# Recurrence heads of a group collected and turned by VectorE one block later, in a fused attention and recurrence block

## The reference

```python
h = rmsnorm(x, norm_gain[l])
proj = jnp.einsum('bsd,dn->bsn', h, w_in[l])
qa, ka, va, za, qb, fb, ib, zb, ga, gb = jnp.split(proj, SPLIT_POINTS, axis=-1)
a = window_sink_attention(qa, ka, va, attn_sinks[l]) * jax.nn.silu(za)
ob = hgrn2_chunkwise(qb, fb, ib, lower_bounds[l])
ob = ob * lax.rsqrt(jnp.mean(ob * ob, axis=-1, keepdims=True) + EPS)
ob = ob.reshape(B, S, HGRN_V_WIDTH) * hgrn_norm_gain[l].astype(jnp.float32)
b = ob.astype(x.dtype) * jax.nn.silu(zb)
y = (jax.nn.sigmoid(ga) * jnp.einsum('bsc,cd->bsd', a, w_up_attn[l])
     + jax.nn.sigmoid(gb) * jnp.einsum('bsc,cd->bsd', b, w_up_hgrn[l]))
x = x + jnp.einsum('bsd,de->bse', y, w_out[l])
```

## Time and profile before

| | |
|---|---|
| Median of 3 runs | 2672.86 us (2672.34 to 2673.23) |
| The profiled execution | 2672.82 us, of which its span of instructions is 2671.0 us |
| TensorE busy | 2642.4 us, 99% |
| VectorE busy | 1740.4 us, 65% |
| ScalarE busy | 1448.0 us, 54% |
| Granted clock of TensorE | 0.998 over the span |

### The profile page before, as it was taken

The page is one execution under the profiler, slowest core; times in us unless marked ns, Lnnn a source line. Parts: engine busy times, 40 slices in busy tenths (PEclk is TensorE's granted clock), DMA queues, the critical chain, the costliest instruction groups (busy, mean ns, idle before and its releaser), DMA issues.

```text
span 2671.0 us, 39981 instructions
## 1 busy us (share of the span) xinstructions
PE 2642.4 (99%) x12049; PEld 2195.7 (82%) x12049; DVE 1740.4 (65%) x3341; ACT 1448.0 (54%) x2420; POOL 0.2 (0%) x4
## 2 busy tenths in 40 slices
PE   8999999999999999999999999999999999999997
PEld 7788888888888888888888888888888888888886
DVE  6566887877877866666555656565656565755554
ACT  5555665656656555555544444444454544554544
POOL 0000000000000000000000000000000000000000
PEclk9999999999999999999999999999999999999999
DMA  7666565665656656666666666666666666676665
GB/s 235 183 194 177 169 183 172 174 182 168 179 173 174 182 173 174 180 177 178 175 189 199 190 195 191 195 190 195 190 195 190 195 191 193 196 221 211 213 214 179
DMA packets 258936, 503.39 MB, mean 188 GB/s; under 512 B 15552, under 2 KB 15760, under 8 KB 258832
## 3 DMA queue, kind: packets, MB, share of 16 engines
q1 hardware_dynamic: 258608, 502.02, 63.0%
q10 hardware_dynamic: 224, 0.03, 0.0%
HBM read 497.80 MB, written 4.19 MB: 188 GB/s over the span
## 4 chain that ended last, share of the span: by engine, by line
PE 97%; DVE 2%; ACT 0%; DMA 0%; issue 0%; SPq 0%; ACTq 0%; DVEq 0%
PE acc L398 31%; PE acc L402 31%; PE acc L399 31%; PE lev L411 1%; DVE w_lo L847 1%; PE lev L413 0%; DVE land_h L855 0%; DMA x_in<-in_x_dram 0%; DVE h_lo L1192 0%; PE mis L424 0%; DVE proj L855 0%; PE mis L458 0%; PE lev L450 0%; ACT w_hi L584 0%; PE outp L435 0%
## 5 line engine op out<-in xcount | busy, mean ns | idle before, releaser
L847 DVE TENSOR_TENSOR w_lo<-raw,w_hi 128x512 fp32r<-128x512 f32 x1856 | 1274.0, 690 | 886.1 <-ACT w_hi L584 880.5
L584 ACT ACTIVATE w_hi<-raw 128x512 fp32r<-128x512 f32 x1856 | 1164.1, 631 | 1166.6 <-PE acc L402 1153.6
L398 PE MATMUL acc<-w_hi,h_hi 128*128 128x512 f32 x3200 | 1263.0, 395 | 2.5 <-ACT w_hi L584 2.5
L399 PE MATMUL acc<-w_hi,h_lo 128*128 128x512 f32 x3200 | 1247.3, 390 | 0.0
L402 PE MATMUL acc<-w_lo,h_hi 128*128 128x512 f32 x3200 | 987.4, 390 | 0.2
L402 PEld LDWEIGHTS acc<-w_lo,h_hi 128*128 128x128 f32 x3200 | 600.4, 188 | 129.1 <-DVE w_lo L847 2.4
L398 PEld LDWEIGHTS acc<-w_hi,h_hi 128*128 128x128 f32 x3200 | 601.5, 188 | 124.0 <-ACT w_hi L584 3.3
L399 PEld LDWEIGHTS acc<-w_hi,h_lo 128*128 128x128 f32 x3200 | 601.7, 188 | 120.9
L398 PE MATMUL acc<-w_hi,a_hi 128*128 128x512 f32 x256 | 99.6, 389 | 0.0
L399 PE MATMUL acc<-w_hi,a_lo 128*128 128x512 f32 x256 | 99.6, 389 | 0.0
L398 PE MATMUL acc<-w_hi,b_hi 128*128 128x512 f32 x256 | 99.6, 389 | 0.0
(11 more groups left out here) (149 smaller groups left out, 1047.2 us busy)
## 6 DMA issues: line engine op xcount, KB each, us to landing
raw<-in_w_in_dram SPq DMA_DIRECT2D x672, 512.0 KB, 3.7
raw<-in_w_out_dram SPq DMA_DIRECT2D x128, 512.0 KB, 3.9
raw<-in_w_up_attn_dram SPq DMA_DIRECT2D x64, 512.0 KB, 3.6
raw<-in_w_up_hgrn_dram SPq DMA_DIRECT2D x64, 512.0 KB, 3.6
xr<-in_x_dram SPq DMA_DIRECT2D x8, 512.0 KB, 4.5
out_dram<-xr SPq DMA_DIRECT2D x6, 512.0 KB, 4.8
x_in<-in_x_dram SPq DMA_DIRECT2D x2, 1024.0 KB, 11.0
fgain<-in_final_norm_gain_dram SPq DMA_DIRECT2D x8, 256.0 KB, 6.0
```

The source lines that it names most:

```text
L398: nc.tensor.matmul(o, l_hi[:, kt, tok], w_hi[:, s, :], start=kt == 0, stop=False)
L399: nc.tensor.matmul(o, l_lo[:, kt, tok], w_hi[:, s, :], start=False, stop=False)
L584: nc.scalar.activation(w_hi[:, k % RING, :], raw[:, (k // 2) % RING, k % 2, :], ACT.Copy).then_inc(hi_ready, 1)
L847: nc.vector.tensor_tensor(w_lo[:, k % RING, :], raw[:, (k // 2) % RING, k % 2, :], w_hi[:, k % RING, :].bitcast(F32), ALU.subtract).then_i ...
```

## The change

**Turning.** The transposes on TensorE at step 28 are left for the last group's four heads alone (`turn_bb`). For groups 0 to 2, `bb` becomes as wide as four heads and each head writes its quarter at step 27. VectorE turns the four together into `land_h` with 16 instructions (`bb_turn`, table `B_TURN`): four at steps 29 to 31 of block 3, one at step 0 and eleven at steps 8 to 11 of the block after it, which is block 0 of the next group or of the last stage. In that block ScalarE waits at step 14 for the turns (`bb_turned`) and rounds one head at each of steps 14 to 17 (`b_rounded`), and VectorE makes the four remainders at steps 28 to 31 (`b_rest`). These replace the two instructions at step 31 of every block.

**Loop.** Group 1 is written out ahead of the loop on TensorE, ScalarE and VectorE, and the loop runs over groups 2 and 3.

**Copies and first group.** ScalarE's copies of `land_h` to `proj` move from step 12 to step 16 (`HG_COPY`), behind the staging, and the staging of q at step 12 of block 2 gets a wait for f's turns of its own. VectorE's waits ahead of the turns move from step 20 to 17. In group 0 the turns have a table of their own (`FIRST_TURN`): two at step 17 and one at each of steps 18 to 31, all in the block in which they begin.

```diff
--- before.py
+++ after.py
@@ -106,11 +106,15 @@
+B_TURN = {29: [0], 30: [1, 2], 31: [3], 0: [4], 8: [5, 6, 7], 9: [8, 9, 10], 10: [11, 12, 13], 11: [14, 15]}
+B_HI_AT = [14, 15, 16, 17]
+B_LO_AT = [28, 29, 30, 31]
+FIRST_TURN = {17: [0, 1], **{k: [k - 16] for k in range(18, KT)}}
 QA_FIRST = {14: [0], 16: [1], 18: [2, 3], 20: [4, 5], 21: [6, 7], 22: [8, 9], 23: [10, 11], 24: [12, 13], 25: [14, 15]}
 QA_FROM = 9
 Y_FROM = 4
 HG_STAGE = 12
-HG_FROM = 20
+HG_COPY = 16
...
@@ -412,7 +416,7 @@
-            def hgrn_side(k, hd, slot, b, groups):
+            def hgrn_side(k, hd, slot, b, groups, turn_bb=False):
@@ -435,10 +439,10 @@
-                if k == 28:
+                if k == 28 and turn_bb:
                     pe.wait_ge(bb_done, hd(1))
                     for t in range(TT):
-                        m = nc.tensor.transpose(mis[:, t * P:(t + 1) * P], bb[:, t, :], ident)
+                        m = nc.tensor.transpose(mis[:, t * P:(t + 1) * P], bb[:, t, b * HD:(b + 1) * HD], ident)
@@ -508,7 +512,8 @@
-            with hinted(pe, GROUPS) as g:
+            hgrn_group(count(0, 4 * KT, 1), 1, count(-GH, GH, 1), 0, True)
+            with hinted(pe, GROUPS, 2) as g:
...
@@ -602,8 +607,11 @@
+                elif b == 0:
+                    stage(turn_h, par, n_end, ACT.Sigmoid)
                 else:
-                    stage(turn_h, par, n_end, ACT.Sigmoid if b == 0 else ACT.Silu)
+                    act.wait_ge(f_turned, g + 1)
+                    stage(turn_h, par, n_end, ACT.Silu)
...
@@ -634,10 +642,17 @@
-                if k == 31:
-                    act.wait_ge(bb_tr, hd(1))
+                if k == 31 and last:
+                    act.wait_ge(bb_tr, b + 1)
                     nc.scalar.activation(b_hi[:, bass.ds(hd(0), 1), :].rearrange("p one t -> p (one t)"), mis[:, 0:SEQ], ACT.Copy,
                                          scale=vec[:, bass.ds(hd(64), 1)]).then_inc(b_hi_done, 1)
+
+            def b_rounded(k, hd):
+
+                if k in B_HI_AT:
+                    u = B_HI_AT.index(k)
+                    nc.scalar.activation(b_hi[:, bass.ds(hd(u), 1), :].rearrange("p one t -> p (one t)"), land_h[:, u, :], ACT.Copy,
+                                         scale=vec[:, bass.ds(hd(u + 64), 1)]).then_inc(b_hi_done, 1)
...
@@ -705,6 +720,8 @@
+                            if b == 0 and k == B_HI_AT[0] and prior is not None:
+                                act.wait_ge(bb_turned, prior[1])
@@ -713,18 +730,22 @@
-                            if b >= 2:
-                                hgrn_copy(b - 2, g, slot)
                             pb = (b - 1) % 4
-                            hgrn_epilogue(pb, pb % 2, n(b * KT), slot if b else prev_slot)
+                            hgrn_epilogue(pb, pb % 2, n(b * KT), slot if b else prev_slot, g)
+                        if k == HG_COPY and b >= 2:
+                            hgrn_copy(b - 2, g, slot)
                         if side:
                             hgrn_side(k, lambda i, b=b: hd(b + i), g, prev_slot, b)
+                        if b == 0 and prior is not None:
+                            b_rounded(k, prior[0])
                         if side or b == 3:
                             hgrn_ahead(k, lambda i, b=b: hd(b + 1 + i))
 
             hgrn_group(count(0), count(-GH, GH, 0), 0, 0, 4, False, first=True)
-            with hinted(act, GROUPS) as g:
-                hgrn_group(count(0, 4 * KT, g), count(-GH, GH, g), g, (g % 2) * 4, ((g + 1) % 2) * 4, True)
+            hgrn_group(count(0, 4 * KT, 1), count(-GH, GH, 1), 1, 4, 0, True)
+            with hinted(act, GROUPS, 2) as g:
+                hgrn_group(count(0, 4 * KT, g), count(-GH, GH, g), g, (g % 2) * 4, ((g + 1) % 2) * 4, True,
+                           (count(-2 * GH, GH, g), g - 1))
...
@@ -854,9 +879,9 @@
-            def hgrn_turn(k, dst, done):
-
-                for i in HG_TURN.get(k, []):
+            def hgrn_turn(k, dst, done, places):
+
+                for i in places.get(k, []):
...
@@ -952,14 +977,29 @@
-                        m = nc.vector.scalar_tensor_tensor(bb[:, t, :], outp[:, t * P:(t + 1) * P], rs[:, t:t + 1],
+                        m = nc.vector.scalar_tensor_tensor(bb[:, t, b * HD:(b + 1) * HD], outp[:, t * P:(t + 1) * P], rs[:, t:t + 1],
                                                            rows(slot + 3)[:, t, b * HD:(b + 1) * HD], ALU.mult, ALU.mult)
                     m.then_inc(bb_done, 1)
-                if k == 31:
+                if k == 31 and last:
                     dve.wait_ge(b_hi_done, hd(1))
                     hi = b_hi[:, bass.ds(hd(0), 1), :].rearrange("p one t -> p (one t)").bitcast(F32)
                     nc.vector.scalar_tensor_tensor(b_lo[:, bass.ds(hd(0), 1), :].rearrange("p one t -> p (one t)"), mis[:, 0:SEQ],
                                                    vec[:, bass.ds(hd(64), 1)], hi, ALU.mult, ALU.subtract).then_inc(b_lo_done, 1)
+
+            def bb_turn(k):
+
+                for i in B_TURN.get(k, []):
+                    m = turn_part(land_h, bb, i)
+                    if i == SUBS * SUBS - 1:
+                        m.then_inc(bb_turned, 1)
+
+            def b_rest(k, hd):
+
+                if k in B_LO_AT:
+                    u = B_LO_AT.index(k)
+                    hi = b_hi[:, bass.ds(hd(u), 1), :].rearrange("p one t -> p (one t)").bitcast(F32)
+                    nc.vector.scalar_tensor_tensor(b_lo[:, bass.ds(hd(u), 1), :].rearrange("p one t -> p (one t)"), land_h[:, u, :],
+                                                   vec[:, bass.ds(hd(u + 64), 1)], hi, ALU.mult, ALU.subtract).then_inc(b_lo_done, 1)
@@ -1041,16 +1081,21 @@
-            def hgrn_group(n, hd, g, slot, prev_slot, side):
+            def hgrn_group(n, hd, g, slot, prev_slot, side, prior=None):
                 for b in range(4):
                     for k in range(KT):
-                        if k == HG_FROM and b == 1:
+                        if k == HG_COPY + 1 and b == 1:
                             dve.wait_ge(staged, g * 2 + 1)
                             if side:
                                 dve.wait_ge(q_ready, g)
-                        if k == HG_FROM and b == 2:
+                        if k == HG_COPY + 1 and b == 2:
                             dve.wait_ge(staged, g * 2 + 2)
                             dve.wait_ge(f_ready, g + 1)
+                        if side and b == 3 and k == min(k for k in B_TURN if k > HG_COPY):
+                            dve.wait_ge(q_ready, g + 1)
+                            dve.wait_ge(bb_done, hd(GH))
+                        if b == 0 and k == B_LO_AT[0] and prior is not None:
+                            dve.wait_ge(b_hi_done, prior(GH))
@@ -1074,37 +1119,48 @@
-                            hgrn_turn(k, land_h, f_turned)
+                            hgrn_turn(k, land_h, f_turned, HG_TURN if side else FIRST_TURN)
                         if b == 2 and k > HG_STAGE or b == 3 and k < HG_STAGE:
-                            hgrn_turn(k, land_h, q_turned)
+                            hgrn_turn(k, land_h, q_turned, HG_TURN if side else FIRST_TURN)
                         if side:
                             hgrn_side(k, lambda i, b=b: hd(b + i), g, prev_slot, b)
+                        if side and b == 3 and k > HG_COPY or prior is not None and b == 0 and k < HG_COPY:
+                            bb_turn(k)
+                        if b == 0 and prior is not None:
+                            b_rest(k, prior)
                         if b == 3:
...
             hgrn_group(count(0), count(-GH, GH, 0), 0, 0, 4, False)
-            with hinted(dve, GROUPS) as g:
-                hgrn_group(count(0, 4 * KT, g), count(-GH, GH, g), g, (g % 2) * 4, ((g + 1) % 2) * 4, True)
+            hgrn_group(count(0, 4 * KT, 1), count(-GH, GH, 1), 1, 4, 0, True)
+            with hinted(dve, GROUPS, 2) as g:
+                hgrn_group(count(0, 4 * KT, g), count(-GH, GH, g), g, (g % 2) * 4, ((g + 1) % 2) * 4, True, count(-2 * GH, GH, g))
 
...
                 for k in range(KT):
-                    if k == HG_FROM and b == 1:
+                    if b == 0 and k == B_LO_AT[0]:
+                        dve.wait_ge(b_hi_done, (GROUPS - 1) * GH)
+                    if k == HG_COPY + 1 and b == 1:
                         dve.wait_ge(staged, 2 * GROUPS + 1)
...
                     if b == 1 and k > HG_STAGE or b == 2 and k < HG_STAGE:
-                        hgrn_turn(k, k_att, k_turned)
+                        hgrn_turn(k, k_att, k_turned, HG_TURN)
                     if b == 3:
...
                                 m.then_inc(qa_ready, 1)
-                    hgrn_side(k, lambda i, b=b: (GROUPS - 1) * GH + b + i, GROUPS, last_set, b)
+                    hgrn_side(k, lambda i, b=b: (GROUPS - 1) * GH + b + i, GROUPS, last_set, b, last=True)
+                    if b == 0 and k < HG_COPY:
+                        bb_turn(k)
+                    if b == 0:
```

(13 more changed lines are left out.)

14 lines of the change are left out of this document (8 added, 6 removed).

## The result

The changed kernel takes 2667.61 us (median of 17 runs, 2666.11 to 2668.08), the kernel before on the same chip 2672.93 (17 runs, 2671.95 to 2673.68). The ratio is 0.998, 95% interval 0.9973 to 0.9986. The gain is 5.32 us where 6.35 was forecast. The profiled execution took 2668.05 us, its span 2665.9.

What follows compares the result with a forecast made beforehand. TensorE, busy 2642.4 of 2671.0 us, was taken as the bound, with slack in the helpers. Sum: 2672.82 - 3.08 - 3.24 - 0.03 = 2666.47, so 2666.5 us, range 2665.5 to 2668.6.

Steps and rivals of the forecast that it cites:

- Stalls of group 0, -3.08: Blocks 2 and 3 of group 0: TensorE's idle time, 2.25 + 0.83 us, was claimed to go entirely.
- Transposes, -3.24: Step 28 on TensorE: twelve of sixteen transpose pairs go, each claimed to give back 0.27 us.
- block 2's small excess: Three blocks 2 lose about 0.01 us each over 48.14; an earlier VectorE chain was claimed to save 0.03.
- The rival by which this time does not come back (2669.7): Something else paces steps 28 to 30, so only 3.08 + 0.03 us is gained; chance 6%.
- VectorE's 48 turns and the wait at step 14, 0: VectorE's 20.9 us of turns and ScalarE's wait in block 0 cost nothing; turns are 1.55 us early, 2.19 more free.
- The upper bound of 2.1 us: Most that VectorE's turns might cost: three times the 0.7 us wait for `w_lo` in the last block with a head.
- The rest, 0: VectorE's other waits, SyncE's transfers and group 1 written out: claimed to add no time.
- The fourth rival: Both terms fail, or writing out group 1 costs as much in code fetching as they give: 2672.8 us, chance 3%.
- the 2667.5 that the forecast took as its line for faster: Whole kernel's time: below this counts as faster, as 0.2% or 5.3 us can be told from no change; chance 0.77.

Runs made afterwards that it cites:

- b_first: Kernel before with only group 0's own turn places, the copies at step 16 and the separate wait for f's turns: 2668.84 us, -3.36 against before.
- a_hgturn0: Changed kernel with group 0's turns back in their old places, the copy still at step 16: 2666.90 us, -5.85 against before.
- b_double: Kernel before with each of the 16 pairs of transposes on TensorE issued twice: 2675.76 us, +3.56 against before.
- a_wait12: Changed kernel with block 0's four b_hi roundings at steps 12 to 15 instead of 14 to 17: 2667.34 us, -5.41 against before.
- b_unroll: Kernel before with only group 1 written out ahead of the loop on TensorE, VectorE and ScalarE: 2672.64 us, +0.44 against before.
- b_pad24: Kernel before with 24 one-column memsets on VectorE in block 1 of group 0: 2672.43 us, -0.16 against before.
- b_pad45: Kernel before with 45 one-column memsets on VectorE in blocks 1 and 2 of group 0: 2674.25 us, +2.05 against before.

## Why the prediction was right, and where its sum was off

**Stalls of group 0, -3.08: right in size, half right in reason.** The two blocks gave 2.25 + 0.83 in the trace, and the part alone gave 3.36 by the medians (b_first). The forecast put it down to turns that end twelve steps before ScalarE asks. a_hgturn0 shows that they need not: with the copy moved, the same late turns cost nothing, because the table load is hidden in the wait.

**Transposes, -3.24: right.** All twelve blocks fell from 48.14 or 48.15 to 47.87, 3.31 us together with block 2's small excess. b_double shows that 0.19 to 0.22 of the 0.27 is work and not a wait; the rest is read from the blocks alone. The rival by which this time does not come back (2669.7) is out.

**VectorE's 48 turns and the wait at step 14, 0: right.** The blocks that carry 41.4 us of VectorE's work last 47.86 us, with TensorE busy throughout. The upper bound of 2.1 us was not touched, and a_wait12 shows more reserve than was counted. The rule of the Trainium skill that the forecast weighed ("VectorE: DVE Perf Modes", sections "The three transpose paths" and "Rules for kernel authors") would have given these tiles to TensorE. Here VectorE paid about 21 us that nobody waited for, and TensorE got 3.24 us back in which it was the bound. The runs do not test the page's unit prices, which are for bf16 tiles. They show that unit prices are not what decides when one engine is full and the other is not.

**Block 2's 0.03:** two blocks went from 48.15 to 47.87; too small to tell.

**The rest, 0: this is the term that was mis-sized.** The forecast said "Writing group 1 out changes no engine's order; block lengths in the loop and in written-out stages agree, so 0". For TensorE's order that is true, and b_unroll measures it. But 429 more instructions in VectorE's program (2502 for 2073) also move all code behind them, and a place at which it waits for its instructions fell between the first two of four scalings in the last microseconds, where nothing covers it: +1.53 there and +0.16 in an output block. The sum with it would be 2666.47 + 1.69 = 2668.16, against 2668.05 of the profiled execution. The medians say a little more, 2.0 us between the changed kernel and the one with 100 memsets on the same chip. The argument "No row shows an issue gap at a seam between loop and written-out code" looked for gaps only where loops begin and end; the late places stand 8 to 128 instructions behind an end. The waits view of before had two "issue" waits of ScalarE, 1.8 and 2.1 us, in straight code, which should have raised the question where VectorE's would come to stand. The fourth rival, the change gives nothing, did name the fetching of code as a price, but as one that would eat both terms.

The measured 2667.61 lies inside the range, whose upper end stood for VectorE's turns and not for this, so that is in part luck. It also lies 0.11 us above the 2667.5 that the forecast took as its line for faster: the missed term is what carried it over.

**Best version.** The changed kernel with 100 idle memsets: 2665.28 and 2665.12 us, 7.31 and 7.63 us or 0.27 and 0.29% under the kernel before. That is the forecast 6.35 with nothing given back, and 1.0 to 1.3 us more. The changed kernel's median shows a like excess: 5.32, where its blocks and end account for 4.63. Where it comes from was not shown; the last section has a candidate.

## What to carry to other kernels

When one engine is the bound everywhere, price a moved piece by the full engine's spacing of steps and by whether the other engine's densest block already survives such a load. If an engine waits and then does several things, put last what frees nobody, and let the activation that needs another table be the one that waits: its load ran ahead of the wait here, inside the idle time. After any edit that changes the number of an engine's instructions ahead of an uncovered stretch, look at "issue" waits at the program's end. Look first at the code just behind a loop's end, where all of VectorE's long ones stood here. A few idle instructions in a slack place can shift them away, and here that was worth about a third of the change.

## What the runs showed of the hardware

**VectorE's instructions arrive in pieces of 128.** In the fourteen profiles of this study VectorE has 16 waits on "issue" of over 1 us, 1.3 to 3.5 us long. All of them stand in front of an instruction whose number leaves 63 when divided by 128: 959, 1343, 1471, 1983, 2111, 2367, 2495 or 2623, by the kernel. ScalarE's waits on "issue" of over 1 us, other than that for its first table load, are ten, 1.7 to 2.0 us long, and stand in front of its instruction 1599 (kernel before) or 1855 (changed), which leave 63 too. The two packets on queue 14 in the stretch above have 8 KB each, which is 64 bytes for each of 128 instructions. Most such boundaries cost nothing: the changed kernel has twenty of them and shows two.

The view of waits does not name every late one. b_double has a gap of 3.5 us in front of instruction 1471, and the kernel before, whose VectorE runs the same program, has one of 3.11 there that the view puts down to ScalarE:

```profile
1268.35 0.60 DVE L988 SCALAR_TENSOR_TENSOR aa<-outp,rden,proj 128x128 f32<-128x128 f32 x2
1272.06 1.90 DVE L847 TENSOR_TENSOR w_lo<-raw,w_hi 128x512 fp32r<-128x512 f32 x3 [3.11 <-ACT w_hi L584]
...
1269.06 0.63 ACT L584 ACTIVATE w_hi<-raw 128x512 fp32r<-128x512 f32 x1 [1.04 <-PE acc L402]
```

ScalarE had the tile ready at 1269.69, and VectorE began 2.4 us later, 1.73 us after a packet on queue 14 had started. b_first has the same gap, 3.11 us. So the place decides here, and the profiles hold 18 late boundaries. All 18 are the first boundary behind the end of a loop, 8 to 128 instructions behind it, and in all 18 VectorE goes on 1.6 to 2.2 us after a packet on queue 14 has started; in 16 of them the packet starts only when VectorE has already stopped. Of the 30 other first boundaries behind a loop's end none has more than 0.7 us of idle time ahead of it. What decides between the 18 and the 30 stays open. In the changed kernel 2367 is 128 behind the end of the last loop but one, and 2495 is 8 behind the end of the last.

The Trainium skill ("Runtime: NRT & Kernel Launch", section "Instruction fetch mechanics") says that an engine fetches its next page while it executes, in blocks of 256 instructions, and that crossing a boundary is mostly hidden. By that the place of the code would be nearly free. The traces agree with "mostly"; here the piece is 128 instructions long, and one that was not hidden cost 1.5 us of each launch.

**A short idle time can be followed by a fall of TensorE's clock for some microseconds.** In two executions, b_pad24 and b_pad45, the granted clock fell to 0.5 (the 1.2 GHz level) soon after the idle of group 0's block 2. In b_pad24 TensorE idled 1.96 us until 126.98, worked at the full clock for 1.2 us more, and then had half of it until just before 131.88. TensorE in b_pad24 behind that idle, and the stretches before, in and after it:

```profile
128.65 0.63 PE L399 MATMUL acc<-w_hi,h_hi 128*128 128x512 f32 x1
129.07 0.63 PE L400 MATMUL acc<-w_hi,h_lo 128*128 128x512 f32 x1
...
131.88 0.39 PE L399 MATMUL acc<-w_hi,h_hi 128*128 128x512 f32 x1
```

```profile
106.00:122.00 16.00, 16.00 (x72) 13.23 (x72) 11.02 (x21) 6.98 (x11) 0.00 (x0) 1.00 0.57 183
128.65:131.21 2.56, 2.56 (x8) 1.97 (x7) 1.50 (x3) 0.63 (x1) 0.00 (x0) 0.50 0.83 246
134.00:150.00 16.00, 16.00 (x72) 13.27 (x71) 9.33 (x16) 7.61 (x12) 0.00 (x0) 1.00 0.57 179
```

A matmul takes 0.63 us instead of 0.39, and the block 47.40 instead of 45.77, 1.6 us more. In the profiles of the kernel before, b_unroll and b_double the same stall of 1.96 us has a clock of 1.00 behind it. These three differ from the two already at the start: their block 0 took 52.3 to 52.4 us, that of the two 51.4 and 51.7. So an execution can pay for this stall twice; how often it does can't be told from five profiles. That the change takes the stall away, and this risk with it, may be why the medians gained 0.6 to 1.3 us more than the profiles' blocks (b_first, the changed kernel and the best version above); it was not shown.
